# Paired attention scores, a plain fp32 compressed layer over column groups, and gates folded into a projection block, in a two-layer decoder kernel

## What is computed

```
proj = x @ w_in[i]
(b_g, c_g, h, q, kc, vc, k_s, v_s, k_w, v_w, gates) = jnp.split(proj, split_points, axis=-1)
...
k_cmp = gelu((blocks(kc) + pe) @ w1[0] + b1[0]) @ w2[0] + b2[0]     # blocks of 32 tokens, stride 16: 15 of them
v_cmp = the same of vc with w1[1], ...                               # w1: 2048 x 256
...
p_cmp, p_slc, p_win = masked softmax of (q . k) for the three branches
out = sigmoid(gates)[0] * p_cmp v_cmp + sigmoid(gates)[1] * p_slc v_s + sigmoid(gates)[2] * p_win v_w
```

## Time and profile before

| what | us |
|---|---|
| median of 3 runs (lowest, highest) | 707.14 (705.29, 708.36) |
| the profiled execution, its own time | 701.97 |
| its span in the profile | 699.5 |
| PE busy, all products | 682.2 (98% of the span) |
| DVE busy | 519.2 (74%) |
| ACT busy | 370.1 (53%) |

### The profile page before, as it was taken

One profiled execution on the slowest core, in us unless ns is written; L12 is line 12 of the kernel. 1 busy time (PEld: TensorE's weight loads), 2 busy tenths in 40 slices (PEclk: granted clock), 3 DMA queues, 4 the chain that ended last, 5 costly groups with the idle time before them and its releaser, 6 DMA issues.

```text
span 699.5 us, 11208 instructions
## 1 busy us (share of the span) xinstructions
PE 682.2 (98%) x4310; PEld 601.3 (86%) x4310; DVE 519.2 (74%) x762; ACT 370.1 (53%) x556; POOL 95.4 (14%) x54
## 2 busy tenths in 40 slices
PE   8999999999999999999999999999999999999995
PEld 5899999888998888888778999987889888888884
DVE  4675768878897777777796467697859877777756
ACT  5664535413875666655346443553248566666630
POOL 0000020230361111110000000204105511111001
PEclk9999999899999999999999999999999999999999
DMA  9982443332865555555348243523357855555301
GB/s 291 316 266 63 138 164 121 121 120 78 286 235 190 198 199 198 204 201 174 103 132 285 66 126 119 180 64 118 121 187 242 294 181 180 181 180 180 120 0 60
DMA packets 87401, 116.81 MB, mean 167 GB/s; under 512 B 5230, under 2 KB 73536, under 8 KB 87360
## 3 DMA queue, kind: packets, MB, share of 16 engines
q1 hardware_dynamic: 85920, 111.85, 47.9%
q10 hardware_dynamic: 1440, 4.39, 1.8%
HBM read 115.19 MB, written 1.05 MB: 166 GB/s over the span
## 4 chain that ended last, share of the span: by engine, by line
PE 90%; DVE 6%; DMA 1%; issue 1%; POOL 1%; ACT 1%; SPq 0%; DVEq 0%; ACTq 0%; POOLq 0%
PE bank L1194 19%; PE bank L1196 18%; PE bank L1195 18%; PE bank L1454 17%; PE bank L1457 9%; PE bank L1279 3%; PE bank L1266 2%; DMA x_tok<-in_x 1%; PE bank L1215 1%; DVE ring_lo L308 1%; DVE x_tok L970 1%; DVE stats L954 1%; DVE x_tok L952 1%; PE bank L1258 1%; DVE x_tok L978 1%
## 5 line engine op out<-in xcount | busy, mean ns | idle before, releaser
L308 DVE TENSOR_TENSOR ring_lo<-raw,ring_hi 128x2048 fp32r<-128x2048 f32 x102 | 232.6, 2284 | 22.6 <-ACT ring_hi L304 22.3
L304 ACT ACTIVATE ring_hi<-raw 128x2048 fp32r<-128x2048 f32 x102 | 194.3, 1908 | 12.9 <-DMA raw<-in_w_in 9.4
L1454 PE MATMUL bank<-xx,ring_hi 128*128 128x512 f32 x512 | 127.8, 391 | 0.0
L1454 PEld LDWEIGHTS bank<-xx,ring_hi 128*128 128x128 f32 x512 | 93.1, 189 | 17.3
L721 POOL COPY step_par<-ffn_par 128x16 f32 (+1 forms) x22 | 64.3, 2927 | 219.4 <-DVE work L989 219.4
L1194 PE MATMUL bank<-xx,ring_hi 128*128 128x256 f32 x320 | 92.4, 289 | 0.0
L1195 PE MATMUL bank<-xx,ring_hi 128*128 128x256 f32 x320 | 90.5, 283 | 0.0
L1196 PE MATMUL bank<-xx,ring_lo 128*128 128x256 f32 x320 | 90.5, 283 | 0.0
L989 DVE SCALAR_TENSOR_TENSOR work<-conv_o,step_par,work 128x254 f32<-128x254 f32 (+1 forms) x128 | 56.2, 481 | 38.4 <-ACT work L560 37.3
L1194 PE MATMUL bank<-ring_hi,xx 128*128 128x512 f32 (+1 forms) x224 | 81.0, 361 | 3.8 <-DVE xx L783 3.8
L1194 PE MATMUL bank<-ring_hi,hTh 128*128 128x512 f32 (+1 forms) x224 | 80.7, 360 | 0.0
(11 more groups left out here) (186 smaller groups left out, 989.6 us busy)
## 6 DMA issues: line engine op xcount, KB each, us to landing
raw<-in_w_up SPq DMA_DIRECT2D x44, 1024.0 KB, 5.2
raw<-in_w_down SPq DMA_DIRECT2D x22, 1024.0 KB, 5.1
raw<-in_w_in SPq DMA_DIRECT2D x21, 1024.0 KB, 5.3
raw<-in_cmp_w SPq DMA_DIRECT2D x8, 1024.0 KB, 5.8
raw<-in_w_out SPq DMA_DIRECT2D x8, 1024.0 KB, 4.8
qkv<-in_ln_g ACTq DMA_DIRECT2D x4, 512.0 KB, 3.6
qkv<-in_ln_b ACTq DMA_DIRECT2D x4, 512.0 KB, 4.9
raw<-in_w_in SPq DMA_DIRECT2D x2, 512.0 KB, 5.0
```

The source lines that it names most:

```text
L304: nc.scalar.activation(ring_hi[slot_of(L, u)][:], raw[raw_of(L, u)][:], ACT.Copy).then_inc(hi_done, 1)
L308: eng.tensor_tensor(ring_lo[slot_of(L, u)][:], raw[raw_of(L, u)][:], ring_hi[slot_of(L, u)][:].bitcast(fp32), ALU.subtract).then_inc(split ...
L1454: pe.matmul(dst[:], wh[:, k, P * c:P * (c + 1)], xx[:, k].rearrange("p a n -> p (a n)"), start=k == 0, stop=False)
```

## The change

- Scores: units are ordered so that the two groups of the same heads follow one another; `scores_pair` issues the two units n and n+1 together, product by product, group 0 (rows 0 to 63, bank 0) and group 1 (rows 64 to 127, bank 1) in turn. It waits for the exponentials of both units before, n-1 the last.
- Compressed first layer: `cmp_hidden` multiplies the raw fp32 weights directly, 16 plain fp32 products of 32 stationary columns; block k goes to output partitions 32(k % 4) to 32(k % 4)+31, so there are four partial sums. `transpose_hidden` becomes a plain fp32 product with a matrix that adds the four. Units 7, 8, 10 and 11 are no longer split, and their raw buffers are given back by PE's last product of the half.
- Gates: their 24 columns become columns 256 to 279 of unit 4's products; the separate product and the transpose go.
- The order tables of ACT and DVE: splits 16 to 19 move up by one or two turns, copies and low parts of the blocks go.

```diff
+def split_no(L, u):
+    return L * (NU - 4) + u - sum(w < u for w in W1_U[0] + W1_U[1])
...
-            for g in range(NG):
-                n = NPAIR // (t + 1)
-                for part in range(t + 1):
+            n = NPAIR // (t + 1)
+            for part in range(t + 1):
+                for g in range(NG):
                     out.append((br, t, g, range(part * n, part * n + n), t + 1))
...
+            def scores_pair(L, n):
+
+                br, t, _, heads, kb = ATT[n]
                 if n == 0:
                     pe.wait_ge(qkT_copied, 3 * L + 3)
-                elif n == 1:
                     pe.wait_ge(blocks_in, 2 * L + 2)
                 else:
-                    pe.wait_ge(exp_done, N_ATT * L + n - 1)
-                rows = slice(HEAD * g, HEAD * (g + 1))
+                    pe.wait_ge(exp_done, N_ATT * L + n)
...
+                    for a, (q, k) in enumerate(((qTh, kTh), (qTh, kTl), (qTl, kTh))):
+                        for g in range(NG):
+                            rows = slice(HEAD * g, HEAD * (g + 1))
+                            pe.matmul(bank[g][:, keys * j:keys * (j + 1)], q[rows, h, tok], k[rows, br, 0:keys],
+                                      start=j + a == 0, stop=False, skip_group_check=True)
...
             def cmp_hidden(L, kv):
 
-                pe.wait_ge(blocks_lo, 2 * L + kv + 1)
+                pe.wait_ge(blocks_in, 2 * L + kv + 1)
                 for half, u in enumerate(W1_U[kv]):
-                    wait_unit(L, u)
-                    wh, wl = w_view(L, u, 8)
+                    pe.wait_ge(raw_in[raw_of(L, u)], 16 * (raw_round(L, u) + 1))
+                    w = raw[raw_of(L, u)][:].rearrange("p (k n) -> p k n", k=8)
                     for j in range(8):
                         k = 8 * half + j
-                        ins = mm3(bank[2 + kv][0:NG * NBLK, 0:CMP_HID], blocks_h[kv][:, k, :], blocks_l[kv][:, k, :],
-                                  wh[:, j, :], wl[:, j, :], k == 0, k == NJ - 1)
-                    free_unit(ins, L, u)
+                        rows = slice(32 * (k % 4), 32 * (k % 4) + 32)
+                        ins = pe.matmul(bank[2 + kv][rows, 0:CMP_HID], blocks[kv][:, k, :], w[:, j, :], start=k < 4, stop=k >= NJ - 4,
+                                        skip_group_check=True)
+                    ins.then_inc(split_done[raw_of(L, u)], 1)
...
-                    ins = pe.transpose(bank[2 + kv][:, 256 + 32 * h:286 + 32 * h], hid[:, P * h:P * (h + 1)],
-                                       ident[0:NG * NBLK, 0:NG * NBLK])
+                    ins = pe.matmul(bank[2 + kv][:, 256 + 32 * h:286 + 32 * h], hid[:, P * h:P * (h + 1)],
+                                    cst[:, C_Q:C_Q + NG * NBLK], start=True, stop=True)
...
-                pe.wait_ge(gate_lo, L + 1)
-                for k in range(KT):
-                    ins = mm3(bank[7][0:NGATE, 0:SEQ], gate_wh[:, k, :], gate_wl[:, k, :], xh[:, k, :], xl[:, k, :],
-                              k == 0, k == KT - 1)
...
-                scores(L, 0)
+                scores_pair(L, 0)
                 cmp_hidden(L, 0)
-                scores(L, 1)
                 transpose_hidden(L, 0)
...
-                    if n < 10:
-                        scores(L, n + 2)
+                    if n < 10 and n % 2 == 0:
+                        scores_pair(L, n + 2)
```

More of the change, by code:

```diff
@@ L186, in build @@
         kTl = sb("kTl", [P, 2, SEQ], f32r)
-        blocks = [part[:, :, :].rearrange("p t f -> p (t f)")[:, 480 * kv:480 * (kv + 1)]
-                  .rearrange("p (j b) -> p j b", j=NJ) for kv in range(2)]
-        hid = sb("hid", [NG * NBLK, CMP_HID])
+        blocks = [part[:, kv, :].rearrange("p (j b) -> p j b", j=NJ) for kv in range(2)]
+        hid = sb("hid", [P, CMP_HID])
         hx = sb("hx", [P, 2, 2 * NBLK])
@@ L306, in split_lo, with kw_pieces @@
         def split_lo(eng, L, u, i=0):
-            eng.wait_ge(hi_done, L * NU + u + 6 * i + 1)
+            eng.wait_ge(hi_done, split_no(L, u) + 6 * i + 1)
             eng.tensor_tensor(ring_lo[slot_of(L, u)][:], raw[raw_of(L, u)][:], ring_hi[slot_of(L, u)][:].bitcast(fp32),
                               ALU.subtract).then_inc(split_done[raw_of(L, u)], 1)
+        def kw_pieces(L):
+            slot, src = slot_of(L, 4), raw[raw_of(L, 4)][:].rearrange("p (k n) -> p k n", k=KT)
+            halves = [r[slot][:, 0:(KT - 1) * (256 + NGATE)].rearrange("p (k n) -> p k n", k=KT - 1) for r in (ring_hi, ring_lo)]
+            return [([h[:, :, 0:256] for h in halves], src[:, 0:KT - 1, :]),
+                    ([h[:, :, 256:] for h in halves], gate_w[:, 0:KT - 1, :]),
+                    ([kw_last[:, a, 0:256] for a in range(2)], src[:, KT - 1, :]),
+                    ([kw_last[:, a, 256:] for a in range(2)], gate_w[:, KT - 1, :])]
         def bcast(ap, axis, shape):
@@ L591, in _ @@
                     x_high(L, XT_BANK, 1, xT_done, xT_hi, (1,))
-                    for u in (2, 3, 4):
+                    for u in (2, 3):
                         split_hi(act, L, u)
+                    split_kw_hi(L)
                 else:
@@ L624, in _ @@
                     nc.scalar.activation(dst.rearrange("p i n -> p (i n)"), src[:], ACT.Copy).then_inc(qkT_hi, 1)
-                for kv in range(2):
-                    act.wait_ge(blocks_in, 2 * L + kv + 1)
-                    nc.scalar.activation(blocks_h[kv], blocks[kv], ACT.Copy).then_inc(blocks_hi, 1)
-                split_hi(act, L, 11)
                 conv_init(L, 0)
@@ L1038, in _ @@
                     x_low(L, XT_BANK, 1, xT_hi, xT_lo[1])
-                split_lo(V, L, 4)
-                dve.wait_ge(gate_hi, L + 1)
-                V.tensor_tensor(gate_wl[:], gate_w[:], gate_wh[:].bitcast(fp32), ALU.subtract).then_inc(gate_lo, 1)
-                for u in (5, 6, 7, 8):
+                dve.wait_ge(hi_done, split_no(L, 4) + 1)
+                for (hi, lo), src in kw_pieces(L):
+                    ins = V.tensor_tensor(lo, src, hi.bitcast(fp32), ALU.subtract)
+                ins.then_inc(split_done[raw_of(L, 4)], 1)
+                for u in (5, 6):
                     split_lo(V, L, u)
@@ L1052, in _ @@
                                     ALU.subtract).then_inc(qkT_copied, 1)
+                V.memset(part.rearrange("p t (j b) -> p (t j) b", j=NJ)[:, :, NG * NBLK:32], 0.0)
                 dve.wait_ge(qkT_done, 4 * L + 4)
@@ L1061, in _ @@
                     ins.then_inc(blocks_in, 1)
-                for kv in range(2):
-                    dve.wait_ge(blocks_hi, 2 * L + kv + 1)
-                    V.tensor_tensor(blocks_l[kv], blocks[kv], blocks_h[kv].bitcast(fp32), ALU.subtract).then_inc(blocks_lo, 1)
-                dve.wait_ge(gates_T, L + 1)
-                chain.mark(V.tensor_scalar(egate[:].rearrange("p t n -> p (t n)"), bank[3][:, 448:448 + TT * NGATE], 1.0, None,
-                                           ALU.add))
+                dve.wait_ge(gates_in, 2 * L + 2)
+                gates = egate[:].rearrange("p t n -> p (t n)")
+                chain.mark(V.tensor_scalar(gates, gates, 1.0, None, ALU.add))
                 conv_gate(L, 0)
                 maxima(L, 0, chain)
-                split_lo(V, L, 10)
                 maxima(L, 1, chain)
                 hidden(L, 0, chain)
-                split_lo(V, L, 11)
                 conv_taps(L, 0, chain)
```

94 lines of the change are left out of this document (42 added, 52 removed).

## The result

The changed kernel takes 708.00 us (median of 18 runs, 705.72 to 712.13). The kernel before took 704.84 us beside it (18 runs, 701.52 to 708.36). The ratio is 1.005 with a 95% interval of 1.0031 to 1.0069: half a per cent slower. A median takes in every execution; a ratio leaves out those over 1.5% above the fastest of their kernel (one of `copy_first`'s four, one of `scores_apart`'s two). The profiled execution has a span of 705.5 us (own time 707.31) against 699.5 us.

What follows compares the result with a forecast made beforehand. The prediction took PE, busy 682.2 of 699.5 us, as the bound. Terms summed to -1.3 us a layer, +0.7 with the clock, +1.4 for both; 703.4 profiled plus 5.2 gave 708.5 us, range 699.5 to 716.

Steps and rivals of the forecast that it cites:

- Gates, -2.5: Gates: 24 separate products and two transposes go, unit 4 gets 24 more columns for 0.5 us; net -2.5 us a layer.
- Hidden layer, -7.6: Compressed first layer: 16 plain fp32 products in four overlapping column groups take 1.9 us each time; -7.6 us a layer.
- Scores, -6.3: Score units: two row halves load and run side by side, pairs taking 1.95 and 1.15 us; -6.3 us a layer.
- Short wait, +0.8: After the hidden layer for kv = 0: PE's transpose waits for ACT's copy, no longer hidden by scores; +0.8 us a layer.
- Long wait, +9.5: After the hidden layer for kv = 1: ACT's copy stands behind late-loaded splits of units 13 and 14; +9.5 us a layer.
- Turns, +4.2: Attention turns 4 to 9: DVE has more to do than PE and pairs wait for both units' exponentials; +4.2 us a layer.
- Clock, +2.0 a layer: After the long wait: PE's granted clock drops to its lower level; +2.0 us a layer, between nothing and 3.2.
- From profile to median, +5.2: Whole kernel: the median of the runs lies 5.2 us above the profiled execution, taking 703.4 to 708.5 us.
- two at a time: Rival, hidden layer: the four column groups run only two at a time; +2.1 us a layer, 712.7 us; 20%.
- row halves don't load side by side: Rival, scores: loads do not overlap, 5.1 of the 6.3 us a layer stay; +8.6, 717 us; 10%.
- nothing overlaps: Rival, hidden layer and scores: no products run side by side, 7.1 us for the hidden layer, about 730 us; 4%.
- The clock holds and DVE keeps up: Rival, turns and clock: no 2.0 clock loss and half of the 4.2, so -3.4 a layer, 700 us; 22%.

Runs made afterwards that it cites:

- copy_first: Changed kernel with ACT's copy of the second hidden layer's result moved ahead of the splits of units 13 and 14; 695.22 us, ratio to before 0.9809.
- scores_apart: Changed kernel with all score products of group 0 ahead of all of group 1 within each pair, not alternating; 712.56 us (2 runs).
- hidden_one_group: Changed kernel with all 16 products of the compressed first layer in column group 0, three partial sums left out; 724.36 us, ratio to before 1.0254.
- single_scores: Changed kernel with the pairing alone undone, one score unit at a time in the places of before; 711.12 us, ratio to before 1.0114.
- best_filled: Changed kernel, hidden copy ahead of splits 12 to 14, splits 16 to 19 as before, plus seven useless products in turn 9's wait; 689.05 us, ratio 0.977.

## Why the prediction was right, and where not

The forecast was 708.5 us, the median is 708.00, and the range held it. The mechanism held: less on PE, and one long wait that takes it back. That the number came within 0.5 us is luck, as the last points say. Step by step:

- **Gates, -2.5.** As forecast, but for a detail: unit 4 with 280 columns took 39.06 - 32.78 = 6.28 us in place of 5.85, +0.43 where I had +0.5.
- **Hidden layer, -7.6.** 1.93 us each, both layers; 1.9 forecast. The four groups run side by side, and `hidden_one_group` shows what they save.
- **Scores, -6.3.** A pair took 55.27 - 53.24 = 2.03 us and 1.14 us with its masks, where I had 1.95 and 1.15; that is -6.2. `single_scores` and `scores_apart` confirm the size as PE's work.
- **Short wait, +0.8.** 0.81 us.
- **Long wait, +9.5.** 9.32 and 9.53 us (9.62 and 10.45 in the second profile). The chain (issue 66.65, splits from 71.89 and 74.84, copy at 76.77) is the one worked out, and `copy_first` shows that the order on ACT makes it.
- **Turns, +4.2.** The waits for exponentials in the turns rose from 1.3 to 7.5 us over both layers, +3.1 a layer. DVE is the bound as said, and the term was a microsecond too high. The working has the added split in turn 5; it stands in turn 4.
- **The rest of the span.** Without the clock the terms gave -1.3 a layer. From the end of one such stretch to the next, layer 0 measured -0.2 and layer 1 -0.2, with the dip of the clock behind the long wait in them, 2.5 and 2.9; so -2.7 to -3.1 without. The sum was 1.5 us a layer too high, most of it the turns' term.
- **Clock, +2.0 a layer.** Behind the wait it was 2.5 and 2.9 us, a little under-sized. The step that failed is the sentence before it: "That cost 7 x 0.45 = 3.2 us", taken as a fixed loss of both kernels. By one kernel's own two profiles the loss in the stretch is 1.7 to 8.9 us a layer (its length times one less the granted clock, which was 0.95 at best and 0.77 at worst).
- **From profile to median, +5.2.** This carried more than it should. It rested on three runs; over 18, before's median is 704.84, not 707.14, 2.9 above its profile. With that the sum would have given 706.3. The forecast is only 0.5 off because a base too high by 2.3 met a sum that had no term for a longer time at the lower clock at the end of the turns. The measured difference of medians is 3.2 us where the forecast had 1.4.

Of those 3.2 us, next to nothing (0.3) lies in the rest of the span, by two profiles of each kernel. So the stretch at the end of the turns is probably longer on average in the changed kernel. Worked back from the medians of the spans on record (702.8 and 706.2, less the rest) it is about 70 us before and 73 after, both inside of what single profiles show. The clocks of all runs point the same way. Of the 29.0 us that the changed kernel loses to the clock in the median, 12 to 14 lie in and behind the two long waits (40 us of layer 0 and 50 of layer 1 in its two profiles); that leaves 15 to 17, against 10.5 before. Why the clock is low for longer there isn't shown. `best_filled` speaks against the wait just ahead of the stretch, and `single_scores` hints at the pairs without showing it. **It stays open.**

Of the rivals, "two at a time", "row halves don't load side by side" and "nothing overlaps" fell with the first profile. "The clock holds and DVE keeps up" fell with the 7.5 us of waits and the clock of 0.65 behind the long one.

## What to carry to other kernels

When an engine's own product gives a buffer back, the load, the split and all that is queued behind the split come into that engine's path: count from the release, and let a small copy that the busy engine needs go ahead of work that waits for a landing. Here that order alone was worth about 13 us. With the copy ahead of one more split and the order of the splits of before, a change that took 31.6 us of products off PE's path and lost 3 gains about 15 (689.94 us). Before paying for fewer products in a stage, look at which engine would set its end: pairing saved 12.4 us of products and about 2 us of time once the long wait was gone. And take two profiles of a kernel before a difference of one per cent is put down to a place.

## What the runs showed of the hardware that was not expected

- Products that alternate between two halves of rows have their weights loaded side by side as well: 128 stationary columns that cost 0.11 us each in one half cost 0.062 in alternation, and 0.10 when the same products come one half after the other. Even then the halves overlap at the seam.
- Plain fp32 products of 32 stationary columns in four column groups overlap nearly in full, 1.93 us for what takes 7.04 in one, and their records start four at a time.
- The granted clock falls to its lower level, 0.5, with PE busy without a gap, behind the end of the turns, and stays there for 3 to 20 us (1.7 and 10.2 us lost at half speed, in the first profile of before and in its second); the same program showed a mean of 0.90 and of 0.71 in the same window. Idle time of 9 us brings it too, each time (0.65 over the next 7 us), and products of no use in that time prevent it (1.00).
